# Summing a modulation vector over partitions with four products in column groups of 32, a copy and four turns, in place of sixteen products of one column

## What is computed

```python
mod_all = jnp.einsum('bd,lde->lbe', jax.nn.silu(c), ada_w) + ada_b[:, None, :]
for i in range(DEPTH):
    shift1, scale1, gate1, shift2, scale2, gate2 = jnp.split(mod_all[i], 6, axis=-1)
    h = _modulate(x, shift1, scale1)
    y = mixer(h)                      # layer 0: RWKV-7 scan, layer 1: sparse attention
    x = x + gate1[:, None, :] * y
    h = _modulate(x, shift2, scale2)
    x = x + gate2[:, None, :] * _swiglu(h, f_w1[i], f_w3[i], f_w2[i])
```

## Time and profile before

| | |
|---|---|
| runs | 2893.86, 2898.17, 2901.64 us, median 2898.17 |
| profiled execution, its own time | 2888.72 us |
| its span in the trace | 2887.1 us |
| TensorE busy (matmul) | 2715.8 us, 94% |
| VectorE busy | 1977.4 us, 68% |
| ScalarE busy | 1326.1 us, 46% |
| mean granted TensorE clock | 0.97 of full speed |
| moved by DMA | 639.99 MB, mean 222 GB/s |

### The profile page before, as it was taken

The page is one execution under the profiler, slowest core; times in us unless marked ns, Lnnn a source line. Parts: engine busy times, 40 slices in busy tenths (PEclk is TensorE's granted clock), DMA queues, the critical chain, the costliest instruction groups (busy, mean ns, idle before and its releaser), DMA issues.

```text
span 2887.1 us, 55171 instructions
## 1 busy us (share of the span) xinstructions
PE 2715.8 (94%) x20665; PEld 2333.5 (81%) x20665; DVE 1977.4 (68%) x2611; ACT 1326.1 (46%) x2022; POOL 45.0 (2%) x89
## 2 busy tenths in 40 slices
PE   7799997888888999999999979988989999999998
PEld 2488886788877888888888868877878888888886
DVE  5678735888767778777777886544767755555556
ACT  2355544444444554344344443344445534444444
POOL 1000001000000000000000000000000000000000
PEclk9999999999999999999999989999999999999999
DMA  9889847443366878788777777632758855665653
GB/s 332 287 275 308 286 140 256 139 148 127 116 216 204 281 263 300 256 281 285 264 272 263 262 247 259 205 98 90 266 181 278 277 182 183 194 188 186 188 168 117
DMA packets 484945, 639.99 MB, mean 222 GB/s; under 512 B 21909, under 2 KB 427834, under 8 KB 468154
## 3 DMA queue, kind: packets, MB, share of 16 engines
q1 hardware_dynamic: 480954, 625.31, 65.2%
q0 software_dynamic: 3840, 12.59, 1.2%
HBM read 623.14 MB, written 14.68 MB: 221 GB/s over the span
## 4 chain that ended last, share of the span: by engine, by line
PE 64%; DVE 5%; ACT 2%; issue 2%; DVEq 0%; ACTq 0%
PE ps L1687 40%; PE ps L1688 20%; DVE wlo L1675 1%; PE ps L1734 1%; PE ps L1363 1%; PE ps L1354 1%; DVE ada_acc L1720 1%; DVE nt L133 1%; ACT whi L1670 1%; DVE act L146 1%; PE ps L1390 0%; PE ps L1756 0%; DVE gsum L100 0%; DVE nt L1431 0%; DVE x L319 0%
## 5 line engine op out<-in xcount | busy, mean ns | idle before, releaser
L1687 PE MATMUL ps<-act,whi 128*128 128x512 f32 x3808 | 1349.7, 399 | 32.8 <-DVE act L146 17.7
L1675 DVE TENSOR_TENSOR wlo<-raw,whi 128x1024 fp32r<-128x1024 f32 (+1 forms) x768 | 901.2, 1192 | 491.2 <-ACT whi L1670 487.7
L1670 ACT ACTIVATE whi<-raw 128x1024 fp32r<-128x1024 f32 (+1 forms) x768 | 774.7, 1030 | 657.9 <-PE ps L1688 654.1
L1688 PE MATMUL ps<-act,wlo 128*128 128x256 f32 x3808 | 1070.9, 281 | 0.0
L1687 PEld LDWEIGHTS ps<-act,whi 128*128 128x128 f32 x3808 | 723.7, 190 | 208.8 <-issue 27.6
L1687 PE MATMUL ps<-hid,whi 128*128 128x512 f32 x2176 | 775.4, 399 | 12.3 <-DVE wlo L1675 9.3
L1688 PEld LDWEIGHTS ps<-act,wlo 128*128 128x128 f32 x3808 | 726.9, 191 | 0.0
L1688 PE MATMUL ps<-hid,wlo 128*128 128x256 f32 x2176 | 615.9, 283 | 0.0
L1687 PEld LDWEIGHTS ps<-hid,whi 128*128 128x128 f32 x2176 | 413.4, 190 | 113.0 <-DVE wlo L1675 11.6
L1688 PEld LDWEIGHTS ps<-hid,wlo 128*128 128x128 f32 x2176 | 412.6, 190 | 0.0
L1720 DVE SCALAR_TENSOR_TENSOR ada_acc<-ada_ring,sc,ada_acc 128x2048 f32<-128x2048 f32 x128 | 300.2, 2346 | 0.3
(11 more groups left out here) (280 smaller groups left out, 2260.9 us busy)
## 6 DMA issues: line engine op xcount, KB each, us to landing
raw<-in_f_w SPq DMA_DIRECT2D x480, 512.0 KB, 4.6
ada_ring<-in_ada_w SPq DMA_DIRECT2D x172, 1024.0 KB, 7.6
raw<-in_a_w_rkv SPq DMA_DIRECT2D x96, 512.0 KB, 5.4
raw<-in_b_w_in SPq DMA_DIRECT2D x56, 512.0 KB, 4.0
raw<-in_f_w SPq DMA_DIRECT2D x64, 384.0 KB, 3.9
first_ring<-in_ada_w SPq DMA_DIRECT2D x20, 1024.0 KB, 11.0
raw<-in_a_w_o SPq DMA_DIRECT2D x32, 512.0 KB, 6.4
raw<-in_b_w_o SPq DMA_DIRECT2D x32, 512.0 KB, 5.5
```

The source lines that it names most:

```text
L1670: self.nc.scalar.activation(self.whi[:, u % SPL, 0:n], self.raw[:, u, 0:n], ACT.Copy).then_inc(self.s("hi_ready"), 1)
L1675: self.nc.vector.tensor_tensor(self.wlo[:, u % SPL, 0:n], self.raw[:, u, 0:n], self.whi[:, u % SPL, 0:n].bitcast(F32), SUB).then_inc(self. ...
L1687: self.nc.tensor.matmul(o, hi[:, kk, c0:c1], src[:, k].rearrange("p a t -> p (a t)"), start=k == 0, stop=False)
L1688: last = self.nc.tensor.matmul(o[:, T:2 * T], lo[:, kk, c0:c1], src[:, k, 0, :], start=False, stop=k == ktotal - 1)
```

## The change

The sum over partitions becomes three steps:

1. `ada_sum`: after unit 3, four products (L1749 of the changed kernel) with 32 columns of ones as weights and 512 columns of `ada_acc` as the moving side. The j-th writes partitions 32j to 32j+31 of bank 7, so each lies in a column group of its own, and every one of its 32 partitions holds the same 512 sums.
2. `ada_row_out`: ScalarE copies bank 7 (128 x 512) to `row` (L1760), after it has split unit 7 and ahead of the copy of group 0 (L95). `row` lies over masks that only the mixer uses; piece 2, ahead of the mixer, uses `ada_acc` itself.
3. `ada_turn`: ahead of unit 5, TensorE turns the four blocks of 128 columns of `row` (L1767) into bank 6. VectorE's `ada_finish` now reads there one column in 32 of the right order.

VectorE has a wait of its own for the products to be done with `ada_acc` (`ada_free`), between units 6 and 7, and `ada_finish` moves behind unit 7. In ScalarE's list the pair with a sum is written out, outside of the loop.

```diff
-        def half(i):
+        def half(i, piece=None):
             for u in range(4, 8):
                 p.split_hi(act, i, u, s0, p0, size)
+            if piece is not None:
+                p.ada_row_out(act, *piece)
             evac.act(act, i, 0, s0 + 4)
...
                 if piece is not None:
-                    p.ada_finish(dve, *piece)
+                    p.ada_free(dve, *piece)
                 if a is not None:
                     if a % 16 == 0 and i is lo:
                         p.ada_zero(dve)
                     p.ada_add(dve, a, i - lo, 0)
                 p.split_lo(dve, i, 7, s0, size)
+                if piece is not None:
+                    p.ada_finish(dve, *piece)
                 evac.dve(dve, i, 0, s0 + 4)
...
                     u = 4 * g + q
+                    if u == 5 and piece is not None:
+                        p.ada_turn(pe, *piece)
                     pe.wait_ge(s("unit_split"), i * 8 + (self.s0 + u + 1))
...
-    def ada_sum(self, pe, piece, n):
+    def ada_sum(self, pe, piece, n, r):
 
         pe.wait_ge(self.s("ada_added"), 16 * (piece + 1))
-        if n > 1:
-            pe.wait_ge(self.s("mod_ready"), n - 1)
-        for m in range(KT):
-            last = self.nc.tensor.matmul(self.ps[:, 7, m:m + 1], self.ada_acc[:, m * P:(m + 1) * P], self.ones[:, 0:1],
-                                         start=True, stop=True)
+        if r > 1:
+            pe.wait_ge(self.s("row_copied"), r - 1)
+        for j in range(4):
+            last = self.nc.tensor.matmul(self.ps[32 * j:32 * j + 32, 7, :], self.ones[:, 0:32], self.ada_acc[:, j * 512:(j + 1) * 512],
+                                         start=True, stop=True, skip_group_check=True)
+        last.then_inc(self.s("row_summed"), 1)
+
+    def row_of(self, piece):
+
+        return self.ada_acc[:, 0:512] if piece == 2 else self.row[:]
+
+    def ada_row_out(self, act, piece, n, r):
+        act.wait_ge(self.s("row_summed"), r)
+        act.wait_ge(self.s("ada_summed"), n - 1)
+        self.nc.scalar.activation(self.row_of(piece), self.ps[:, 7, :], ACT.Copy).then_inc(self.s("row_copied"), 1)
+
+    def ada_turn(self, pe, piece, n, r):
+
+        pe.wait_ge(self.s("row_copied"), r)
+        pe.wait_ge(self.s("mod_ready"), n - 1)
+        for m in range(4):
+            last = self.nc.tensor.transpose(self.ps[:, 6, m * P:(m + 1) * P], self.row_of(piece)[:, m * P:(m + 1) * P], self.ident[:])
         last.then_inc(self.s("ada_summed"), 1)
 
-    def ada_finish(self, dve, piece, n):
+    def ada_free(self, dve, piece, n, r):
+
+        dve.wait_ge(self.s("row_summed"), r)
+
+    def ada_finish(self, dve, piece, n, r):
         dve.wait_ge(self.s("ada_summed"), n)
         sl = slice(16 * piece, 16 * piece + 16)
-        bias = self.pv[:, PV_ADA + 16 * piece:PV_ADA + 16 * piece + 16]
-        self.nc.vector.tensor_tensor(self.mod[:, sl], self.ps[:, 7, 0:16], bias, ADD).then_inc(self.s("mod_ready"), 1)
+        bias = self.pv[:, PV_ADA + 16 * piece:PV_ADA + 16 * piece + 16].rearrange("p (j m) -> p j m", j=4)
+        sums = self.ps[:, 6, :].rearrange("p (m j r) -> p j m r", m=4, j=4)[:, :, :, 0]
+        self.nc.vector.tensor_tensor(self.mod[:, sl].rearrange("p (j m) -> p j m", j=4), sums, bias, ADD).then_inc(self.s("mod_ready"), 1)
```

More of the change, by code:

```diff
@@ L478, in half, with body @@
                 m.beside_act(act, i, 0)
-        def body(i):
-            half(i)
+        def body(i, piece=None):
+            half(i, piece)
             for u in range(4):
@@ L488, in scalar @@
             body(0)
-        self.over(act, 0 if s0 else 1, n - 1, body)
-        half(n - 1)
+        at = 0 if s0 else 1
+        for b in sorted(self.sums):
+            if b < n - 1:
+                self.over(act, at, b, body)
+                body(b, self.sums[b])
+                at = b + 1
+        self.over(act, at, n - 1, body)
+        half(n - 1, self.sums.get(n - 1))
         if self.ahead:
@@ L1487, in __init__ @@
         self.ada_sums = 0
+        self.row_sums = 0
         self.rows_done = None
@@ L1542, in layout @@
         self.centre64 = head("centre64")
+        self.row = nc.alloc_sbuf_tensor_at("row", [P, 512], F32, offset=at[0] - HD * 4)
         two = lambda name: place(name, [P, 2, HD])[0]
@@ L1725, in take_piece @@
         self.ada_sums += 1
-        return piece, self.ada_sums
-    def ada_sum(self, pe, piece, n):
+        self.row_sums += 1
+        return piece, self.ada_sums, self.row_sums
+    def ada_sum(self, pe, piece, n, r):
         pe.wait_ge(self.s("ada_added"), 16 * (piece + 1))
-        if n > 1:
-            pe.wait_ge(self.s("mod_ready"), n - 1)
-        for m in range(KT):
-            last = self.nc.tensor.matmul(self.ps[:, 7, m:m + 1], self.ada_acc[:, m * P:(m + 1) * P], self.ones[:, 0:1],
-                                         start=True, stop=True)
+        if r > 1:
[4 more added lines that the diff above has]
+        last.then_inc(self.s("row_summed"), 1)
@@ L2482, in build @@
         phases += [loras, self.rwkv(loras)]
-        for name in ("squared", "square_added", "sums_zeroed", "x_added", "normed", "sigmoid", "silu", "hid_hi", "cleared"):
+        for name in ("squared", "square_added", "sums_zeroed", "x_added", "normed", "sigmoid", "silu", "hid_hi", "cleared", "row_summed", "row_copied"):
             self.s(name)
```

## The result

The changed kernel took 2865.99 us, the median of four runs (2860.68 to 2870.06); the kernel before, in four runs beside it, 2897.78 (2893.86 to 2901.64). The ratio is 0.9896, with a 95% interval of 0.9875 to 0.9917. It is faster by about 30 us (31.8 between the medians), where 18 were forecast; the time lies 2 us under the low end of the range and 3.7 us under the rival "all four groups at once".

The account below looks back on a forecast made before the run. TensorE, busy for 94% of the span, was taken as the bound, with each sum on its path. Sums falling from 41.2 to 23.0 us save 18.2, giving 2870.5 for the profiled execution, 2880.0 carried to the median; range 2868 to 2893.

Parts of the forecast that it names:

- all four groups at once: Rival at the eight sums: all column groups start together, products 0.86 us, 1.59 a piece, total 2869.7 us; chance 0.09.
- What the sums cost before: On TensorE, the eight old sums with the slow steps behind them were read to cost 41.2 us.
- The term 2.14: At each piece's four products: staggered passes fill five slots of 0.429 us, 2.14 us in all.
- The switches: TensorE going in and out of column groups: 0.1 us each, 0.2 for the two at a piece.
- The turn: Four records of 128 columns on TensorE: 0.44 us, and 0.09 for the first step behind them.
- The sum: One piece on TensorE after the change: 2.14 + 0.20 + 0.44 + 0.09 = 2.87 us, eight of them 23.0.
- The clock: Behind the sums: streaming 512 columns leaves no drop to half clock, so its 12.6 us go.
- the clock still falls: Rival behind the sums: all half-clock drops stay, so the saving is 5.6 us and the time 2892.6; chance 0.14.
- its rival: At the turns: if transposes don't count as TensorE activity, part of the clock drops would come back; no separate chance.
- The groups don't overlap: Rival at the four products: groups run in sequence, 4.16 us a piece, saving 7.9, total 2890.3; chance 0.16.
- Slower: Rival at the sums: groups in sequence plus a long clock drop every piece, 7.3 us each, total 2915; chance 0.05.
- The copy and the waits: ScalarE's copy ends 2 us before the turn; VectorE runs 1 us late in three pieces, covered by over 3 us: nothing.

## Why the prediction was wrong, step by step

**What the sums cost before.** Right: 41.2 us read, 40.8 to 42.6 by three readings. Read as "behind piece 2, but not behind piece 10", the clock's part was also right as a sum and wrong as a list of places, since the places change between executions.

**The step that failed.** "First pass of group 0, then its second pass beside the first of group 1, and so on. Four groups then take five slots and not two." It was argued from the order of issue and from quadrant rows in which two records run at a time. The trace after has all four first passes start within 0.05 us (some 7 ns from one to the next) and the second passes 0.45 us later: two slots of 0.45. The term 2.14 was mis-sized by more than a factor of two; with its switches it measured 1.09 where 2.34 stood. The runs with eight and with seven products show it as a mechanism and not as a lucky piece: +0.87 for four products in four groups, +2.58 for three in one, and 3.59 us for eight passes in the whole array. The Trainium skill ("TensorE: Matmul & The Clock Gate", Part 3), with small products in different tiles starting a few ns apart and four costing little more than one, agrees with this trace for float32 as well, pass by pass. The 0.86 us that the prediction worked out by it stands against 0.90 measured. I had both numbers, gave the row of two quadrants more weight than it can bear (it holds only two groups, so it can't show four), and left the case a chance of 0.09.

**The switches**, 0.2 a piece: measured 0.09 going in and 0.10 coming out. Right, but the 0.10 of the first step behind comes on top of them. **The turn**, 0.44 and 0.09: measured 0.36 and 0.08.

**The sum.** 2.87 a piece and 23.0 in all were forecast, 1.63 and 13.0 measured. The saving at the pieces is 28 to 29.6 instead of 18.2. Measured savings, from the ratios times 2893, are 30, 26 and 26 us in three series.

**The clock.** Right, and tested two ways: no drop behind four groups, behind one group alone, or behind four and five turns; and behind the old products, cut in two lots of eight, there is none either. (A wait of 1.78 us in that kernel did have one behind it, a wait of 1.72 us with the late turn had none.) The rival "the clock still falls" is out. The Trainium skill (same page, Part 4) says that transposes don't count as activity; no drop follows turns of 0.36 or 0.47 us amid the big products, so its rival had nothing to give here, and no run has a longer stretch of them.

**The groups don't overlap** was the changed kernel without column groups: 3.87 a piece, 4.16 foreseen, and no measurable gain left. **Slower** needed sequence and long drops together; neither came.

**The copy and the waits.** Right. The copy starts 0.07 us after the products' last record ends, and ends 2 us before the turn. VectorE waits for the turn in pieces 2, 10 and 11 (6.0 us) and nobody waits for VectorE: TensorE's waits for `wlo` are 13.6 us against 14.2. The evacuation at piece 10 starts 4.6 us after the sum's start, against 4.9 before and 5.9 foreseen, since the products ended 1.2 us sooner. Both edges of the cover were found: the turn directly behind the products adds 0.76 us a piece, two units later it adds waits at the phase's head.

**The range.** Its low end, 2868, was the rival's own time less 1.7 us, with no room for the spread of the runs, which was 9.4 us over the four of the changed kernel. The base of the sum, 2898.17, was the median of three runs; the four beside the result gave 2897.78, so it is not what put the time under the range, though 61 later runs gave medians of 2890 to 2892. Without its failed term the forecast would have been 2869.7, inside the range and still 3.7 above the result.

## What to carry to other kernels

Sums over partitions that are written as one-column products with 128 columns of weights cost 0.109 us a record here, and in most places they also pulled TensorE's clock down behind them; turned round and spread over the four column groups the same sum costs 1.63 us with its turn instead of 3.58, and the clock stays. A row that shows two things running at once bounds how four would run and doesn't say it: where a rule speaks for more overlap, its time belongs inside the range with a chance of weight, not at the edge. Put other work between the products and whatever reads them, but not too much: here one unit hid the copy, none cost 0.76 us a piece, and three cost some 10 us in waits over the eight pieces.

## What the runs showed of the hardware that was not expected

**Four column groups run at once, pass by pass.** Float32 products take two passes of 0.43 to 0.45 us for 512 columns. Four groups take the same two slots as one, and passes in one group queue behind each other.

**The big products keep two paces.** With the granted clock at 1.00 and no wait, a step of 512 + 256 columns takes about 347 or about 353 ns, the same for a hundred steps and more. Records of the 512-column product alone, in 500 us of the last phase, of before and of the one with VectorE's transposes:

```profile
2345.00:2845.00 500.00, 500.00 (x1438) 269.73 (x1437) 1.00 0.60 186
```

```profile
2330.00:2830.00 500.00, 500.00 (x1416) 265.94 (x1416) 1.00 0.56 176
```

500 / 1438 is 348 ns and 500 / 1416 is 353; the changed kernel has 1433 there in all three of its profiles, 349 ns. That is a mixture. Its pace changes four times inside this stretch, with no wait and no step over 358 ns; two windows of 76 us in the changed kernel:

```profile
2390.00:2466.00 76.00, 76.00 (x221) 41.03 (x220) 1.00 0.61 190
2560.00:2636.00 76.00, 76.00 (x217) 40.43 (x216) 1.00 0.60 188
```

So a pace can change without a disturbance of TensorE. The same two paces show between pieces 6 and 7, before (463 records in 160 us) and after (454):

```profile
1224.00:1384.00 160.00, 160.00 (x463) 86.28 (x462) 1.00 0.84 284
```

```profile
1218.00:1378.00 160.00, 160.00 (x454) 85.12 (x453) 1.00 0.83 285
```

Of the 5984 steps some 5850 start within 0.4 us of the one before; over these a mean longer by 1 ns is 5.9 us. It is 349.9 and 350.3 in two profiles of before, 350.7, 350.8 and 351.0 in three of the changed kernel, 351.8 with eight products and 352.0 without column groups. By that the changed kernel would give back some 4 us in its steps, and the kernels without column groups and with eight products come out near what was measured (-10 at the pieces and +11, measured -3.7; -21 and +10, measured -12.7). But this account does not hold for all kernels: the mean is 351.8 with VectorE's transposes and 351.9 with the late turn, where pieces and steps together would give 22 and 8 us less than before, and 34 and 18 were measured. The mixer's stretch alone differs by more from profile to profile (406.4 to 420.5 us over all thirteen). So what the steps cost in all is not shown, and the 28 to 29.6 us at the pieces agree with the 26 to 30 measured, within their intervals, without it.

The stretches mostly fall alike in repeated profiles of one kernel, but not always. The stretch from 1700 is at 347 and the next at 353 in one profile of the changed kernel, and the other way round in the second. Of the five stretches that the third profile of the changed kernel was to repeat, four did, and the one behind piece 5 had 347.9 ns in place of 352.9. With the fifth turn the stretches behind pieces 6 and 7 stayed as they were, and the last one changed a little, to 1439 records in 500 us, 348 ns in place of 349. That decides for none of the ideas written down ahead of it. What chooses the pace is open; no run was made that sets it.
